# Page loads of the first two cached batches, released by groups of prompt score heads

## The chip, the cores and the metric

The kernel runs on one core of one Trainium2 chip. The metric is the device time of one execution in microseconds (us); lower is better. A core has a matrix engine (PE, TensorE), a vector engine (DVE), a scalar engine (ACT), a general engine (POOL, GpSimd) and a queue engine (SP), each with its own in-order instruction stream. They meet only at semaphores. SBUF is the on-chip memory (128 partitions), PSUM the accumulators of PE (8 banks).

## The reference, cut to what matters

One inference step of two layers. Layer 0 mixes tokens by multi-head latent attention, layer 1 by gated linear attention, and each has a feed-forward half before and after. 512 prompt tokens and 8 sample batches of 8 new tokens go through the same weights. The change lies in layer 0's attention, between these two parts:

```python
# prompt: 512 queries x 512 keys, 8 heads
s = (jnp.einsum('bqhd,bkhd->bhqk', qn, k_nope)
     + jnp.einsum('bqhr,bkr->bhqk', qp, k_pe)).astype(jnp.float32) * MLA_SCALE
p = jax.nn.softmax(s, axis=-1)
o = jnp.einsum('bhqk,bkhd->bqhd', p, v)
...
# sample: every batch reads 16 pages of 128 cached positions through its page table
past_ckv = cache_ckv[page_table].reshape(B, -1, MLA_KV_LORA)   # 256 wide
past_kpe = cache_kpe[page_table].reshape(B, -1, MLA_ROPE)      # 64 wide
```

## The kernel before, in words

Six stages run in turn: feed-forward, `mla`, feed-forward, feed-forward, `gla`, feed-forward. Activations lie transposed in SBUF; weights stream through four slots `raw`, which SP loads, ACT and POOL split into high and low parts, and PE multiplies three times (lines 1550 to 1552).

The `mla` stage has projections, then the prompt attention, then the sample attention, then the output product. In the prompt attention PE works through 32 windows (8 heads `hd` of 4 query blocks). For window `w` it computes `scores(w)` from `qn[:, hd]`, `kn[:, hd]` and `qpe[:, hd]` (lines 1789, 1790, the last raises `s_s`), DVE and ACT do the softmax (DVE lines 1245, 1248, 1250, 1255, 1258, ACT line 708), PE transposes the probabilities `prob` (line 1815), ACT copies them to `pt` (line 720), and once a head PE multiplies with the values `vp` (line 1797, which raises `s_o`). The scores run two windows ahead of the transposes.

In the sample attention the 8 batches go in 4 pairs `bp`. A batch has 16 pages of 128 positions x 320 numbers, 160 KB each, and four buffers `cache0` to `cache3` hold two pairs. A pair is worked in 4 groups `g` of 4 pages. PE transposes one batch's group (lines 1844 and 1847, `transpose_pages(x)`, x counting batch-groups: 0 and 1 are group 0 of batches 0 and 1, 2 and 3 are group 1, and so on, 8 a pair), ACT (line 734) and DVE (line 1268) copy it out, PE computes the group's scores (lines 1860, 1862); after four groups come the exponentials, their transposes (`fill`, line 1883) and the product with the pages (line 1916, which raises `s_pvg` once a group).

The buffers overlay what is dead by then. `qn` begins at `g_at` and takes 8 rows of `W4` = 2304 bytes per partition, one a head; `qpe` takes the next 8; `kn` and then `vp` follow. `cache0` takes bytes 0 to 20479 from `g_at`, `cache1` 20480 to 40959, so these two lie on `qn`, `qpe` and the first two heads of `kn`; `cache2` and `cache3` lie on the rest of `kn`, on `vp` and on what is beyond.

Each page is one DMA. SP issues two pages of every group of four, POOL the other two, both through `load_pages`, a loop that reads the page number from `table` and issues. PE waits, before a group's transposes, for all of its pages (lines 1835, 1836). Ahead of `load_pages` in SP's stream stand the weight loads up to the third block of the output product; behind it stand the load of `uv_f` and the other output weights. On POOL the splits of the projections' weights stand ahead and those of the output weights behind.

Of the kernel before, what the change touches and what calls it, by code (L numbers as in the profile page):

```python
# [27 lines left out]
HEADS, NOPE, ROPE, VD = 8, 128, 64, 128  # L28
Q_LORA, KV_LORA = 384, 256
QT, KT = Q_LORA // P, KV_LORA // P  # L30
N_POOL, PAGE, PAST = 160, 128, 2048
PAGES = PAST // PAGE
# [3 lines left out]
QB = SEQ // P  # L36
# [31 lines left out]
def hybrid_step(nc, io, stages=STAGES):  # L68
    pre_gain = PRE_GAIN
    post_gain = [None] + POST_GAIN  # L70
    with ExitStack() as ctx:
        def sem(name):
            return ctx.enter_context(nc.semaphore(name))
# [46 lines left out]
        W4 = TOK * 4  # L120
# [115 lines left out]
        s_out = sem("s_out")  # L236
# [5 lines left out]
        s_s, s_msk, s_max, s_neg = sem("s_s"), sem("s_msk"), sem("s_max"), sem("s_neg")  # L242
        s_exp, s_rec, s_pn, s_t, s_pt = sem("s_exp"), sem("s_rec"), sem("s_pn"), sem("s_t"), sem("s_pt")
        s_o, s_ohi, s_olo = sem("s_o"), sem("s_ohi"), sem("s_olo")
# [7 lines left out]
        s_pvg, s_rowt, s_rows, s_ckvs, s_masks = (sem(x) for x in ("s_pvg", "s_rowt", "s_rows", "s_ckvs", "s_masks"))  # L252
# [108 lines left out]
        def load_pages(eng, u0, landed, lo, hi):  # L361

            eng.wait_ge(s_table, 16)

            eng.wait_ge(s_o, HEADS)
            eng.wait_ge(s_evicted, u0 + M_O)
            eng.wait_ge(s_qpes, HEADS)
            eng.wait_ge(s_ckvs, 1)
            eng.wait_ge(s_out, 32)
            for bp in range(PAIRS):  # L370
                for g in range(GROUPS):
                    if 2 * bp >= CACHES:

                        eng.wait_ge(s_pvg, GROUPS * (bp - CACHES // 2) + g + 1)
                    for b in (2 * bp, 2 * bp + 1):
                        with eng.Fori(lo, hi) as i:
                            page = eng.value_load(table[0:1, bass.ds(PAGES * b + 4 * g + i, 1)], min_val=0,
                                                  max_val=N_POOL - 1)
                            eng.dma_start(cache[b % CACHES][:, 4 * g + i, :],  # L379
                                          io["cache"][page]).then_inc(landed[bp % (CACHES // 2)][g], 16)  # L380
# [28 lines left out]
        def _(sp):  # L409
# [33 lines left out]
            def mla(st):  # L443
# [25 lines left out]
                for j in range(MLA_IN + HEADS, MLA_BLOCKS - DT + SLOTS - 1):  # L469
                    load_n(j)  # L470

                load_pages(sp, u0, s_cache, 0, SP_PAGES)

                sp.wait_ge(s_pvg, GROUPS * (PAIRS - 1))
# [396 lines left out]
        def _(pool):  # L871
# [22 lines left out]
            def mla(st):  # L894
                n0 = first_block[st]
                pool.wait_ge(s_lo, n0 + SLOTS)
                for j in range(4, MLA_BLOCKS - DT):
                    low(n0 + j)
                load_pages(pool, first_unit[st], s_cache_p, SP_PAGES, 4)
                for j in range(MLA_BLOCKS - DT, MLA_BLOCKS - DT + 3):  # L900
                    low(n0 + j)
                mix_out(st, n0 + MLA_BLOCKS - DT)
# [1302 lines left out]
```

## Time and profile before

| | |
|---|---|
| median of 3 runs | 2523.54 us (2517.78 to 2524.62) |
| the profiled execution, its own time | 2515.44 us |
| its span in the trace | 2513.8 us |
| PE busy | 2439.3 us, 97% of the span |
| DVE, ACT, POOL busy | 1019.4, 789.8, 852.2 us |
| granted PE clock, mean | 0.99 |

The span runs from the first to the last instruction; the execution's own time is 1.6 us longer. All times inside the program are from the start of the span. The views of the trace used below are the page's summary, a table of stretches (busy time of each engine, granted clock and DMA share), the engines' timelines, the chain that ended last, the waits, and the groups of instructions by shape.

### The profile page before, as it was taken

The page shows a single profiled execution, that of the slowest core. Times are in us where ns is not written, and L with a number is a line of the kernel's source. Part 1 is how long each engine was busy: PE and PEld are TensorE (multiplying, and loading weights), DVE is VectorE, ACT ScalarE, POOL GpSimd, SP SyncE. Part 2 cuts the span into 40 slices and gives each one's busy share as a digit, 9 for nine tenths or more (in the row PEclk, how much of TensorE's full clock was granted, in tenths as well). Part 3 has the DMA queues.
Part 4 walks back from the last instruction along what each step waited for, and adds up shares of the span by engine and source line. Part 5 has one row for each costly group of instructions (what it writes and reads, how often), then busy time and mean ns, then how long its engine had stood idle before and what let it go on. Part 6 is the DMA issues. An engine that isn't in the chain of part 4 may idle for free.

```text
span 2513.8 us, 43938 instructions
## 1 busy us (share of the span) xinstructions
PE 2439.3 (97%) x17572; PEld 2299.7 (91%) x17572; DVE 1019.4 (41%) x1919; ACT 789.8 (31%) x1392; POOL 852.2 (34%) x477
## 2 busy tenths in 40 slices
PE   8999999899899999999999999999999999999997
PEld 8999999895456999999999999999988799999997
DVE  5332222686332643332254332126577666323223
ACT  5222222414332442222243222224321444222221
POOL 3333333120221133333314333331467423333332
PEclk9999999999999999999999999999999999999999
DMA  3222222130551232222213222222211322222222
GB/s 123 84 84 83 80 84 80 58 115 1 164 172 34 60 91 80 81 83 85 82 58 96 84 80 81 83 86 78 68 51 51 143 85 68 84 83 83 79 86 76
DMA packets 68648, 209.04 MB, mean 83 GB/s; under 512 B 8380, under 2 KB 21181, under 8 KB 68254
## 3 DMA queue, kind: packets, MB, share of 16 engines
q1 hardware_dynamic: 65438, 196.58, 25.5%
q0 software_dynamic: 3072, 10.49, 1.5%
q8 instruction: 103, 1.69, 0.3%
q14 instruction: 35, 0.29, 0.0%
HBM read 199.22 MB, written 7.82 MB: 82 GB/s over the span
## 4 chain that ended last, share of the span: by engine, by line
PE 88%; DVE 8%; ACT 1%; issue 1%; POOL 1%; DMA 0%; POOLq 0%; SPq 0%; DVEq 0%
PE psum L1550 25%; PE psum L1552 25%; PE psum L1551 25%; PE psum L1844 1%; PE psum L1860 1%; DVE h L1016 1%; PE psum L1916 1%; DVE y_ffn L1012 1%; PE psum L1998 1%; DVE x_lo L986 1%; PE psum L1790 1%; DVE work L1007 1%; PE psum L1789 1%; PE psum L1797 1%; DVE w_lo L995 1%
## 5 line engine op out<-in xcount | busy, mean ns | idle before, releaser
L875 POOL TENSOR_TENSOR w_lo<-raw,w_hi 128x1024 fp32r<-128x1024 f32 (+2 forms) x315 | 734.7, 2334 | 1420.0 <-ACT w_hi L526 1420.0
L1550 PE MATMUL psum<-x_hi,w_hi 128*128 128x288 f32 x3568 | 1072.9, 301 | 21.9 <-DVE x_lo L986 17.7
L1552 PE MATMUL psum<-x_hi,w_lo 128*128 128x288 f32 x3568 | 1053.9, 295 | 0.0
L1551 PE MATMUL psum<-x_lo,w_hi 128*128 128x288 f32 x3568 | 1052.9, 295 | 0.0
L1550 PEld LDWEIGHTS psum<-x_hi,w_hi 128*128 128x128 f32 x3568 | 671.7, 188 | 38.5 <-DVE x_lo L986 27.4
L1551 PEld LDWEIGHTS psum<-x_lo,w_hi 128*128 128x128 f32 x3568 | 671.9, 188 | 3.7
L1552 PEld LDWEIGHTS psum<-x_hi,w_lo 128*128 128x128 f32 x3568 | 671.4, 188 | 0.0
L526 ACT ACTIVATE w_hi<-raw 128x1024 fp32r<-128x1024 f32 (+2 forms) x331 | 341.4, 1033 | 797.9 <-DMA raw<-ffn_in 364.2
L1032 DVE TENSOR_TENSOR work<-psum,r_pre 128x288 f32<-128x288 f32 x352 | 160.3, 457 | 659.5 <-PE psum L1552 659.0
L1550 PE MATMUL psum<-gu_hi,w_hi 128*128 128x288 f32 x1408 | 415.5, 295 | 0.0
L1552 PE MATMUL psum<-gu_hi,w_lo 128*128 128x288 f32 x1408 | 414.7, 295 | 0.0
L1551 PE MATMUL psum<-gu_lo,w_hi 128*128 128x288 f32 x1408 | 414.6, 294 | 0.0
L1550 PEld LDWEIGHTS psum<-gu_hi,w_hi 128*128 128x128 f32 x1408 | 264.2, 188 | 0.2
L1551 PEld LDWEIGHTS psum<-gu_lo,w_hi 128*128 128x128 f32 x1408 | 264.1, 188 | 0.2
L1552 PEld LDWEIGHTS psum<-gu_hi,w_lo 128*128 128x128 f32 x1408 | 264.1, 188 | 0.0
L1037 DVE COPY y_ffn<-psum 128x288 f32 (+1 forms) x60 | 27.1, 452 | 366.9 <-PE psum L1552 366.9
L565 ACT ACTIVATE gu_hi<-work 128x288 f32 (+1 forms) x176 | 76.9, 437 | 224.6 <-DVE work L1053 224.6
L1053 DVE TENSOR_TENSOR work<-work 128x288 f32<-128x288 f32 x176 | 116.0, 659 | 28.6 <-ACT work L561 11.5
L561 ACT ACTIVATE work<-work 128x288 f32<-128x288 f32 x176 | 76.3, 436 | 134.0 <-DVE work L1032 133.9
L1048 DVE TENSOR_TENSOR acc<-acc,work 128x288 f32<-128x288 f32 x68 | 89.7, 1319 | 67.2 <-ACT work L570 67.2
L1057 DVE TENSOR_TENSOR gu_lo<-work,gu_hi 128x288 f32 (+1 forms) x176 | 79.3, 453 | 27.8 <-ACT gu_hi L565 26.1
L379 POOL DMA_DIRECT2D cache<-cache x64 | 34.5, 539 | 163.9 <-issue 162.9
(262 smaller groups left out, 1928.4 us busy)
## 6 DMA issues: line engine op xcount, KB each, us to landing
raw<-ffn_in SPq DMA_DIRECT2D x176, 512.0 KB, 3.6
raw<-ffn_out SPq DMA_DIRECT2D x64, 448.0 KB, 3.3
raw<-ffn_out SPq DMA_DIRECT2D x32, 512.0 KB, 3.5
raw<-gla_in SPq DMA_DIRECT2D x25, 512.0 KB, 3.6
cache<-cache SPq DMA_DIRECT2D x64, 160.0 KB, 3.0
cache<-cache POOLq DMA_DIRECT2D x64, 160.0 KB, 3.1
raw<-mla_wo SPq DMA_DIRECT2D x8, 512.0 KB, 3.6
raw<-gla_wo SPq DMA_DIRECT2D x8, 512.0 KB, 3.5
```

What stands on the lines that cost most here:

```text
L379: eng.dma_start(cache[b % CACHES][:, 4 * g + i, :], io["cache"][page]).then_inc(landed[bp % (CACHES // 2)][g], 16)
L526: act.activation(w_hi[slot][:, 0:w], raw[slot][:, 0:w], ACT.Copy).then_inc(s_hi, 1)
L561: act.activation(work[:, hf, :], work[:, hf, :], ACT.Silu).then_inc(s_silu, 1)
L565: act.activation(gu_hi[:, i, H[hf]], work[:, 2 + hf, :], ACT.Copy).then_inc(s_guhi, 1)
L875: pool.tensor_tensor(w_lo[slot][:, 0:w], raw[slot][:, 0:w], w_hi[slot][:, 0:w].bitcast(F32), ALU.subtract).then_inc(s_lo, 1)
L1032: dve.tensor_tensor(dst, bank[bk][0:r, 0:HALF], r_pre[0:r, H[hf]], ALU.mult).then_inc(s_evicted, 1)
L1048: dve.tensor_tensor(acc[:, H[hf]], acc[:, H[hf]], work[:, hf, :], ALU.add).then_inc(s_acc, 1)
L1053: dve.tensor_tensor(work[:, 2 + hf, :], work[:, hf, :], work[:, 2 + hf, :], ALU.mult).then_inc(s_gu, 1)
L1057: dve.tensor_tensor(gu_lo[:, pi, H[hf]], work[:, 2 + hf, :], gu_hi[:, pi, H[hf]].bitcast(F32), ALU.subtract).then_inc(s_gulo, 1)
L1550: pe.matmul(out, wh, xh, start=start, stop=False)
L1551: pe.matmul(out, wh, xl, start=False, stop=False)
L1552: return pe.matmul(out, wl, xh, start=False, stop=stop)
```

## The change

The six waits that stood ahead of all page loads are split. Three of them (`s_table`, `s_evicted`, `s_qpes`) stay where they were. The other three (`s_o` at 8 heads, `s_ckvs`, `s_out`) move to the first load of batch 2. Each group's loads of batches 0 and 1 get a wait of their own, on the number of prompt score windows done.

```diff
-            eng.wait_ge(s_o, HEADS)
             eng.wait_ge(s_evicted, u0 + M_O)
             eng.wait_ge(s_qpes, HEADS)
-            eng.wait_ge(s_ckvs, 1)
-            eng.wait_ge(s_out, 32)
+
+            def last_head(b, g):
+
+                page_w = (KV_LORA + ROPE) * 4
+                held = range((b * PAGES + 4 * g) * page_w // W4, ((b * PAGES + 4 * g + 4) * page_w - 1) // W4 + 1)
+                return max(x % HEADS if x < 2 * HEADS else HEADS - 1 for x in held)
+
             for bp in range(PAIRS):
                 for g in range(GROUPS):
                     if 2 * bp >= CACHES:
 
                         eng.wait_ge(s_pvg, GROUPS * (bp - CACHES // 2) + g + 1)
                     for b in (2 * bp, 2 * bp + 1):
+                        if b < 2:
+                            eng.wait_ge(s_s, QB * (last_head(b, g) + 1))
+                        if (b, g) == (2, 0):
+                            eng.wait_ge(s_o, HEADS)
+                            eng.wait_ge(s_ckvs, 1)
+                            eng.wait_ge(s_out, 32)
                         with eng.Fori(lo, hi) as i:
```

In the order of issue, (group 0, batch 0), (0, 1), (1, 0), (1, 1), (2, 0), (2, 1), (3, 0), (3, 1), the new waits are for `s_s` at 12, 16, 20, 24, 28, 32, 32, 32 of 32 windows.

POOL's stream before, at the start of the page loads (`w_lo`, `raw`, `w_hi` are slots of the last projection weights; `cache_107` and `cache_108` are `cache0` and `cache1`, `cache_109` and `cache_110` are `cache2` and `cache3`):

```order
L875 TENSOR_TENSOR w_lo_59<-raw_55,w_hi_63 128x1024 [waits s_hi]
L376 UNCONDITIONAL_BRANCH [waits s_qpes,s_ckvs,s_evicted,s_out,s_o,s_table]
L376 ISA
L377 TENSOR_LOAD table
L377 ISA x2
L379 ISA
L379 DMA cache_107<-cache 128x320
L376 REGISTER_ALU
L376 COMPARE_AND_BRANCH
L376 UNCONDITIONAL_BRANCH
```

The same place of POOL's stream in the change:

```order
L885 TENSOR_TENSOR w_lo_59<-raw_55,w_hi_63 128x1024 [waits s_hi]
L386 UNCONDITIONAL_BRANCH [waits s_qpes,s_s,s_evicted,s_table]
L386 ISA
L387 TENSOR_LOAD table
L387 ISA x2
L389 ISA
L389 DMA cache_107<-cache 128x320
L386 REGISTER_ALU
L386 COMPARE_AND_BRANCH
L386 UNCONDITIONAL_BRANCH [waits s_s]
```

No instruction is added or moved: each loop's first branch now carries the wait for `s_s`, and `s_o`, `s_ckvs` and `s_out` are gone from the first. SP's stream changes in the same way, and the streams of PE, DVE and ACT are what they were.

POOL's stream in the change at the last load of batch 1 and the first of batch 2:

```order
L386 UNCONDITIONAL_BRANCH [waits s_s]
L386 ISA
L387 TENSOR_LOAD table
L387 ISA x2
L389 ISA
L389 DMA cache_108<-cache 128x320
L386 REGISTER_ALU
L386 COMPARE_AND_BRANCH
L386 UNCONDITIONAL_BRANCH [waits s_out,s_ckvs,s_o]
```

Here the three waits have come to stand, ahead of `cache_109`; in the kernel before this last branch had no wait.

## Rows read from the trace of the kernel before

**Rows 1.** The page, chain that ended last, shares by engine

```profile
PE 88%; DVE 8%; ACT 1%; issue 1%; POOL 1%; DMA 0%; POOLq 0%; SPq 0%; DVEq 0%
```

**Rows 2.** Stretches: us, busy PE, PEld, DVE, ACT, POOL; clock, DMA share, GB/s

```profile
646.00:648.00 2.00, 0.00 (x0) 0.00 (x0) 0.00 (x0) 0.00 (x0) 0.92 (x2) 0.50 0.70 215
...
654.00:656.00 2.00, 1.95 (x10) 1.39 (x8) 0.69 (x1) 0.63 (x3) 0.79 (x2) 0.51 0.74 234
656.00:658.00 2.00, 1.47 (x12) 1.26 (x12) 0.69 (x1) 0.94 (x2) 0.54 (x1) 1.00 0.63 202
```

**Rows 3.** PE timeline, prompt attention to pair 0: start, duration, instruction, idle before

```profile
588.50 1.12 PE L1790 MATMUL psum<-kpe,qpe 64*128 64x512 f32 x2
...
633.40 1.12 PE L1790 MATMUL psum<-kpe,qpe 64*128 64x512 f32 x2
...
638.70 2.42 PE L1797 MATMUL psum<-pt,vp 128*128 128x512 f32 x8 [0.69 <-ACT pt L720]
642.54 0.41 PE L1827 MATMUL psum<-ident,ckv_s 128*64 128x128 f32 x2 [1.41 <-DVE x_lo L1236]
650.60 1.94 PE L1844 MATMUL psum<-ident,cache 128*128 128x128 f32 x8 [7.65 <-DMA cache<-cache]
...
656.53 1.06 PE L1844 MATMUL psum<-ident,cache 128*128 128x128 f32 x8 [0.58 <-issue]
...
662.92 1.06 PE L1844 MATMUL psum<-ident,cache 128*128 128x128 f32 x8 [0.51 <-issue]
...
680.54 2.66 PE L1883 MATMUL psum<-ident,p_s 128*128 128x128 f32 x16 [0.37 <-ACT p_s L748]
```

**Rows 4.** PE timeline, last product of pair 0 and pair 1

```profile
684.44 7.13 PE L1916 MATMUL psum<-cache,pt_s 128*64 128x256 f32 x64
...
692.08 1.09 PE L1844 MATMUL psum<-ident,cache 128*128 128x128 f32 x8
...
695.04 1.94 PE L1860 MATMUL psum<-c_t,q_lat 128*64 128x512 f32 x8
...
713.19 1.09 PE L1844 MATMUL psum<-ident,cache 128*128 128x128 f32 x8
...
715.60 2.66 PE L1883 MATMUL psum<-ident,p_s 128*128 128x128 f32 x16 [0.37 <-ACT p_s L748]
```

**Rows 5.** POOL timeline, page issues: 1st, 4th, 8th and 33rd of 64

```profile
643.00 0.74 POOL L379 DMA_DIRECT2D cache<-cache  x1 [94.50 <-issue]
...
647.62 0.54 POOL L379 DMA_DIRECT2D cache<-cache  x1 [1.00 <-issue]
...
653.72 0.54 POOL L379 DMA_DIRECT2D cache<-cache  x1 [1.01 <-issue]
...
692.42 0.54 POOL L379 DMA_DIRECT2D cache<-cache  x1 [0.99 <-PE psum L1916]
```

**Rows 6.** Chain that ended last, in time, at the first pages

```profile
647.62 2.84 DMA cache<-cache
```

**Rows 7.** SP's waits between 560 and 800 us: total, times, longest

```profile
SPq L369 <- PE psum L1797: 72.4, 1, 72.4
```

**Rows 8.** Groups by shape, 575 to 640 us: busy, mean ns, idle before

```profile
L1815 PEld LDWEIGHTS psum<-ident,prob 128*128 128x128 f32 x75 | 8.1, 140 | 12.6 <-DVE prob L1258 11.3 <-issue 0.5
...
L1248 DVE TENSOR_REDUCE soft<-psum 128x1 f32<-128x512 f32 x7 | 4.8, 691 | 0.2
...
L1258 DVE TENSOR_SCALAR prob<-prob,soft 128x512 f32<-128x512 f32 x8 | 3.9, 487 | 0.3
```

**Rows 9.** Groups by shape, DVE, 642 to 750 us

```profile
L1292 DVE TENSOR_REDUCE mx<-psum 128x1 f32<-128x512 f32 x12 | 8.3, 692 | 32.3 <-PE psum L1862 32.3
```

**Rows 10.** Groups by shape, DVE, feed-forward, 200 to 450 us

```profile
L1048 DVE TENSOR_TENSOR acc<-acc,work 128x288 f32<-128x288 f32 x12 | 15.5, 1291 | 11.3 <-ACT work L570 11.3
...
L1016 DVE TENSOR_TENSOR h<-h,y_ffn 128x288 f32<-128x288 f32 x8 | 3.6, 456 | 0.0
```

**Rows 11.** PE timeline, pair 3

```profile
785.74 3.58 PE L1883 MATMUL psum<-ident,p_s 128*128 128x128 f32 x16 [0.37 <-ACT p_s L748]
```

## The prediction, made before the changed kernel had run

> **What bounds the kernel now.** First the chain that ended last: 88% of the span is PE's own work [rows 1], so a change pays only where PE stands still or runs slowly. The changed waits hold back page loads, so I went next to the place where PE meets the first pages. PE's timeline shows the last value product of the prompt attention, from 638.70 to 641.12, then 1.41 us of idleness and two small transposes that end at 642.95, and then 7.65 us in which PE waits for a page DMA [rows 3]. Seek three things there. The first is that hole. The second is in the table of stretches: in the hole the granted clock falls to 0.50, that is from 2.4 to 1.2 GHz, it is still 0.51 at 654 to 656 us, and it is 1.00 again from 656 us [rows 2]. The third is two gaps, 0.58 us before 656.53 and 0.51 us before 662.92, both before a new group's transposes [rows 3].
>
> What is late in all of them is POOL's share of the pages. POOL issues its first page at 643.00, 1.9 us after the last value product ended, the fourth at 647.62 and the eighth at 653.72 [rows 5], so one each 1.53 us ((653.72 - 643.00) / 7). The chain names the fourth POOL issue and 2.84 us to its landing [rows 6]: group 0 is complete at 650.46, and PE starts at 650.60. Group 1 is complete at 653.72 + 2.84 = 656.56, and PE starts its next group at 656.53. Group 2 comes four issues later, about 662.7, against 662.92. So the two "issue" gaps are page waits too. Group 3 would land at about 668.8. From there on PE is not held by pages: pair 1 shows no gap before its transposes [rows 4].
>
> **The change part by part.** No instruction is added; eight waits for `s_s` on each of two queues cost nothing, since these stand still anyway (SP has waited 72.4 us for the value products [rows 7]). All that changes is when the loads may start.
>
> *Batches 0 and 1.* PE's rows date the semaphore: the fourth window of head 2 ends at 588.50 + 1.12 = 589.6 and that of head 7 at 633.40 + 1.12 = 634.5, five heads apart, so a head takes 8.98 us [rows 3]. The waits at 12, 16, 20, 24, 28 and 32 windows open at 589.6, 598.6, 607.6, 616.5, 625.5 and 634.5. POOL's first issue comes 1.9 us later. Groups 0 and 1 and half of group 2 lie in SBUF before 634.5. Then POOL has six issues left: the first at 636.4, the last at 636.4 + 5 x 1.53 = 644.1, landed at 646.9.
>
> *What PE then does.* It ends the small transposes at 642.95 and goes straight on, at the full clock. Two batch-groups of transposes take 695.04 - 692.08 = 2.96 us in pair 1 [rows 4], and from the first of these, the ones of the pair's second group, it is 715.60 - 692.08 = 23.52 us to the fills [rows 4]. Pair 0 first has its group 0 and then this same stretch. For pair 0: 642.95 + 2.96 = 645.91, + 23.52 = 669.43, against 680.54 now [rows 3]: **11.1 us** earlier. By terms: 7.65 us of hole; the first two batch-groups took 656.53 - 0.58 - 650.60 = 5.35 us instead of 2.96, so 2.4 us of half clock; and 0.58 + 0.51 = 1.1 us of gaps. Sum 11.1 us, both ways.
>
> *What is late next.* Group 3 is needed three groups of work after the start, about 658, and is there at 646.9. Batch 2 and 3 loads now queue behind the six late issues: POOL gets to them at 645.6. Before, they were the 17th issue, at 643.00 + 16 x 1.53 = 667.5, so they come 22 us earlier. Their group 0 has landed at about 645.6 + 3 x 1.53 + 2.84 = 653.0. PE wants it where x 8 is transposed. That is the counterpart of 713.19 in pair 1, one pair period (715.60 - 680.54 = 35.1 us) earlier and 11.1 us shifted, so 667.0: 14 us to spare. Their 16 issues end near 668.5. Pair 2 needs the first quarter of pair 0's product, at 684.44 + 1.8 - 11.1 = 675.1. POOL is free by then, where before it reached this load only at 692.42 [rows 4, 5]. It lands near 684 and is wanted at 713.19 - 11.1 = 702.1. Pair 3 has the same relation to pair 1's product as before. No new page wait follows, and what comes after (`uv_f`, output weights) hangs on semaphores of the sample attention and shifts with it. All later stages start 11.1 us earlier.
>
> *What I can't read off.* POOL now issues 16 page DMAs while DVE and ACT do the prompt softmax. PE is full there, but not by a wide margin: its weight loads waited 11.3 us in all for DVE's scaled `prob` [rows 8], so a late DVE operation reaches PE almost at once. The lower bound of the cost is 0: DVE's maximum over 512 columns takes 691 ns in the quiet attention [rows 8] and 692 ns while pages stream [rows 9], so the traffic alone stretches nothing. The upper bound: each of the 16 issues holds up a DVE operation for its whole 0.54 us [rows 5], 8.6 us. That POOL and DVE can hurt each other is in the feed-forward: the same 128x288 add takes 1291 ns as `acc` and 456 ns as `h` [rows 10]. I take 0.2 us, since POOL's issues follow a head's last score by 1.9 us and 3.4 us, and the `prob` scaling is on for only 0.49 us each time [rows 8]; this is the nearest to the lower end.
>
> A rule of the Trainium skill speaks against the change at this point. Its page "SBUF — State Buffer", section "Who interferes with whom", says that a tensor_scalar in a two-port mode and GpSimd's writing of descriptors for its DMAs lock each other out for a whole instruction. No row shows the two together, since before the change POOL issued nothing in the attention. By the rule alone the sum would lie between 11.1 and 2.5 us, depending on how often they meet.
>
> *The clock.* The fills of pair 3 took 3.58 us [rows 11], those of pair 1 2.66 us [rows 4], so the clock was low once more near 785 us. With everything shifted by 11 us this may come or not come there, or in one of the other short gaps at the end of the stage. I count 0.9 us either way.
>
> **Sum.** 11.1 - 0.2 = 10.9 us. The profiled execution has 2515.44 us and would have 2504.5. It is 8.1 us under the median of the runs shown, so I put the saving on the median: 2523.54 - 10.9 = 2512.6 us, ratio 0.9957.
>
> **The rivals.** (1) *The port.* DVE and POOL meet, and PE's chain stretches by 3 to 8.6 us. For it: the add of 1291 ns [rows 10]. Against: few meetings, and the two engines must coincide within half a microsecond. Time 2515.5 to 2521. (2) *The wait only moves.* The pages are there, but PE is then held by the copies of ACT and DVE, or pair 1 waits for its pages. Against: pair 1 does the same work at 23.52 us with no gap [rows 4], and 14 us are spare. If pair 0 kept its old length from first transpose to fill (680.54 - 650.60 = 29.94 us), only the hole would be won: 2523.5 - 7.7 = 2515.9. (3) *Slower.* The streaming pages stretch the attention itself, by PE's operand reads or all engines. From 589.6 to 641.1 it has 51.5 us; it loses the 11.1 us from a stretch of 22% on and is slower by over 0.3% from 36% (18.7 us) on; 40% would give 2523.5 + 20.6 - 11.1 = 2533. Against: the equal 691 and 692 ns [rows 8, 9]. (4) *It does nothing*, as when a wait stays behind another queue entry. Against: in both streams only the loads stand there, and the kept waits were met before the attention. 2523.5.
>
> **How the numbers follow.** Forecast 0.76, port 0.10, moved wait 0.08, nothing 0.03, slower 0.03. A measurement of this kernel tells about 0.3%, 7.6 us, from no change. The forecast is past it by 3.3 us, and the shown runs are 6.8 us apart, so I leave it a few in a hundred on the wrong side: faster 0.79, same 0.18, slower 0.03. The range: down to 2504 for runs that fall as low as the profiled one (2504.5), up to 2520 for most of the port's cases and the moved wait.
>
> **What would show it.** Right: page issues on SP and POOL from about 591 us in five steps of 9 us; PE's transposes of `cache` start at 643 with no DMA wait; the clock stays at 1.00 between 642 and 658; fills of pair 0 at about 669.4; 8.98 us a head as before. Wrong: a head period above 9.0 us, DVE lines 1258 or POOL's issues longer than 487 and 540 ns, a DMA wait at x 8, or a new clock drop.

## The result, and the profile after

The changed kernel takes 2509.56 us (median of 4 runs, 2509.07 to 2510.05), the kernel before in the same session 2524.08 us (median of 4, 2517.78 to 2525.13). The ratio is 0.9946, with a 95% interval of 0.9933 to 0.9959. That is a saving of 14.5 us between the medians and of 13.6 us by the ratio, where 10.9 us were forecast; the forecast ratio of 0.9957 lies inside the interval. The profiled execution took 2509.59 us with a span of 2507.9 us.

PE's timeline of the changed kernel at the places of [rows 3] and [rows 4] (start, duration, instruction, idle before; the change moves line numbers by 10):

```profile
591.72 1.12 PE L1800 MATMUL psum<-kpe,qpe 64*128 64x512 f32 x2
...
636.62 1.12 PE L1800 MATMUL psum<-kpe,qpe 64*128 64x512 f32 x2
...
641.93 2.42 PE L1807 MATMUL psum<-pt,vp 128*128 128x512 f32 x8 [0.69 <-ACT pt L730]
645.76 0.41 PE L1837 MATMUL psum<-ident,ckv_s 128*64 128x128 f32 x2 [1.41 <-DVE x_lo L1246]
646.01 1.04 PE L1854 MATMUL psum<-ident,cache 128*128 128x128 f32 x8
...
649.05 1.06 PE L1854 MATMUL psum<-ident,cache 128*128 128x128 f32 x8
...
654.86 1.09 PE L1854 MATMUL psum<-ident,cache 128*128 128x128 f32 x8
...
670.14 1.09 PE L1854 MATMUL psum<-ident,cache 128*128 128x128 f32 x8
...
672.54 2.66 PE L1893 MATMUL psum<-ident,p_s 128*128 128x128 f32 x16 [0.37 <-ACT p_s L758]
...
707.61 2.66 PE L1893 MATMUL psum<-ident,p_s 128*128 128x128 f32 x16 [0.37 <-ACT p_s L758]
```

The hole of 7.65 us and both small gaps are gone; PE goes from the small transposes straight to the pages. The stage before the attention happened to run 3.2 us later than in the profile of before, so I measure from inside: from the start of the last value product to the fills of pair 0 it is 672.54 - 641.93 = 30.61 us, against 680.54 - 638.70 = 41.84 [rows 3]. This stretch is called **the page stretch** below. It is 11.2 us shorter. The heads take (636.62 - 591.72) / 5 = 8.98 us as before, and the pairs 35.1 us.

POOL's timeline shows the page issues: the first of group 0 for batch 0 and for batch 1, the first after the last score, and the first issues of batch 2 and of pair 2 (that is, of batches 4 and 5).

```profile
594.76 0.74 POOL L389 DMA_DIRECT2D cache<-cache  x1 [43.99 <-issue]
...
603.27 0.54 POOL L389 DMA_DIRECT2D cache<-cache  x1 [6.40 <-issue]
...
639.19 0.54 POOL L389 DMA_DIRECT2D cache<-cache  x1 [6.92 <-issue]
...
648.47 0.54 POOL L389 DMA_DIRECT2D cache<-cache  x1 [1.08 <-issue]
...
679.84 0.54 POOL L389 DMA_DIRECT2D cache<-cache  x1 [7.34 <-issue]
```

The first issue comes 1.9 us after the twelfth window's score (591.72 + 1.12). The later waits cost less: the last one opens at 636.62 + 1.12 = 637.74 and its issue follows 1.45 us later. The table of stretches (us; busy PE, PEld, DVE, ACT, POOL; granted clock, DMA share, GB/s) has the full clock where [rows 2] had half of it:

```profile
646.00:648.00 2.00, 1.93 (x18) 1.69 (x17) 1.11 (x2) 0.92 (x2) 0.54 (x1) 1.00 0.73 230
654.00:656.00 2.00, 2.00 (x14) 1.19 (x13) 1.00 (x2) 0.01 (x1) 0.54 (x1) 1.00 0.71 209
```

What remained open was the difference between 11.2 us in the page stretch and 13 to 14.5 us in the medians of this run and its repeat (e3). The intervals of both ratios hold the 0.9956 that 11.2 us alone would give, so no single run shows that difference clear of the noise. All runs together do suggest it: 86 executions of the kernel before, in five sessions, have a mean of 2522.5 us and the nine of the change one of 2509.5, which is 13.0 us.

### The profile page after: what moved, and what is told of

Same layout as the page of the kernel before. It is cut to its first block, busy times and chain, and to the rows that moved or that the text cites. A ratio compares the mean times of both kernels' runs of the same rounds, so it can differ in the third digit from the quotient of the medians.

```text
span 2507.9 us, 43938 instructions
## 1 busy us (share of the span) xinstructions
PE 2440.0 (97%) x17572; PEld 2300.2 (92%) x17572; DVE 1021.7 (41%) x1919; ACT 789.6 (31%) x1392; POOL 852.7 (34%) x477
## 4 chain that ended last, share of the span: by engine, by line
PE 88%; DVE 8%; ACT 1%; POOL 1%; issue 1%; DMA 0%; SPq 0%; DVEq 0%; POOLq 0%
PE psum L1560 25%; PE psum L1562 25%; PE psum L1561 25%; PE psum L1870 1%; PE psum L1854 1%; DVE h L1026 1%; PE psum L1926 1%; DVE y_ffn L1022 1%; DVE x_lo L996 1%; PE psum L1800 1%; DVE work L1017 1%; PE psum L2008 1%; PE psum L1799 1%; PE psum L1807 1%; DVE w_lo L1005 1%
## 5 line engine op out<-in xcount | busy, mean ns | idle before, releaser
L1560 PEld LDWEIGHTS psum<-x_hi,w_hi 128*128 128x128 f32 x3568 | 672.4, 188 | 37.6 <-DVE x_lo L996 27.4
L1063 DVE TENSOR_TENSOR work<-work 128x288 f32<-128x288 f32 x176 | 116.2, 660 | 28.3 <-ACT work L571 11.2
```

Of the source, the lines that this page charges most:

```text
L1063: dve.tensor_tensor(work[:, 2 + hf, :], work[:, hf, :], work[:, 2 + hf, :], ALU.mult).then_inc(s_gu, 1)
L1560: pe.matmul(out, wh, xh, start=start, stop=False)
```

## The experiments

Beside the page stretch a second length turned out to matter, **the stage's end**: from the start of the fills of pair 3 to the first matmul of line 1578 (line numbers of the kernel before), a sum of squares near the end of the output product; the expectations call it the first sum of squares. It holds the same work in all kernels but e10 and e11, which have more. The two lengths are read from one profiled execution of each kernel, the medians from all executions. The ratios are not quotients of the medians; for e12 these would give 0.9974. All times in us:

| kernel | median | ratio to before, 95% | page stretch | stage's end |
|---|---|---|---|---|
| before, the profile of [rows 3] | | | 41.84 | 64.3 |
| the change | 2509.56 | 0.9946 [0.9933, 0.9959] | 30.61 | 66.4 |
| e1, before again | 2522.65 | 1.0004 [0.9994, 1.0014] | 42.04 | 70.1 |
| e2, same streams, late loads | 2524.92 | 1.0006 [0.9997, 1.0016] | 42.21 | 70.1 |
| e3, the change again | 2509.07 | 0.9952 [0.9937, 0.9966] | 30.63 | 65.8 |
| e4, one release | 2517.46 | 0.9978 [0.9968, 0.9989] | 36.53 | 70.0 |
| e5, first group only | 2519.61 | 0.9984 [0.9971, 0.9997] | 37.63 | 70.1 |
| e6, POOL issues all | 2508.78 | 0.9952 [0.9938, 0.9966] | 30.62 | 65.8 |
| e7, before, hole filled | 2522.55 | 0.9998 [0.9986, 1.0011] | 42.42 | 68.8 |
| e8, change + 80 transposes | 2520.28 | 0.9991 [0.9978, 1.0004] | 39.36 | 64.3 |
| e9, change + 40 | 2515.93 | 0.9967 [0.9952, 0.9983] | 34.99 | 68.8 |
| e12, change + 20 | 2516.64 | 0.9966 [0.9952, 0.9980] | 32.81 | 70.1 |
| e10, change, end gaps filled | 2507.72 | 0.9940 [0.9923, 0.9956] | 30.63 | 63.3 |
| e11, before, end gaps filled | 2519.94 | 0.9990 [0.9979, 1.0001] | 42.63 | 63.3 |

**e1: the kernel before against itself.** No edit.

> The kernel before, unchanged, timed against itself. Theory (the change saves some 11 us and what the medians show beyond that, 14.5 us, is the scatter of whole executions): ratio 1.000 within 0.002, but single runs between about 2515 and 2525 us, and the stretch from the start of the last value product (line 1797) to the fills of pair 0 (line 1883) stays at 41.8 us whatever the whole time is. Rival (the kernel before is always near 2524 and the profiled 2515 was a freak): all runs within 2 us of 2524.

The kernel before scattered from 2518.35 to 2526.91 us, so the profile of before, at 2515.44, was a low one. Its span here is 2522.7 us, 8.9 more. That splits up: 1.3 ahead of the attention, 0.2 in the page stretch, 5.8 at the stage's end, and 1.6 after it. The page stretch hardly moves; the rest does.

**e2: the streams of the change without the early start.**

```diff
                     for b in (2 * bp, 2 * bp + 1):
+                        if (b, g) == (0, 0):
+                            eng.wait_ge(s_o, HEADS)
                         if b < 2:
```

> The change, but the first page load also waits for all eight heads' value products, so that no load starts earlier than before; the instruction streams are those of the change. Theory (only the earlier start pays): ratio 1.000, last value product to fills 41.8 us as before. Rival (the other shape of the streams is itself worth the 3 us by which the medians exceed the sum): about 2521 us, ratio 0.9987, with the difference ahead of the prompt attention.

Nothing is won, neither in time nor in the page stretch. The gain needs the early loads; the shape of the streams gives none that shows.

**e3: the change again.** No edit.

> The change itself, timed again in more rounds. Theory: last value product to fills 30.6 us, 11.2 less than before, ratio near 0.9956. Rival (some 3 us more are really won elsewhere): ratio 0.9945 or lower, and a second place in the trace where it is always shorter than the kernel before.

The page stretch is 30.63 us, and the five runs lie within 3 us (2507.87 to 2510.79), where those of the kernel before spread over 11 (2516.59 to 2527.41). The ratio came out as 0.9952 with 0.9956 inside its interval, so this run alone leaves both theories standing. The trace has the second place, the stage's end.

**e4: one release for all eight groups.**

```diff
                         if b < 2:
-                            eng.wait_ge(s_s, QB * (last_head(b, g) + 1))
+                            eng.wait_ge(s_s, ATT)
```

> The change, but all eight groups of batches 0 and 1 wait for the scores of all 32 windows, not head by head. POOL would start 1.9 us after 634.5 on the clock of the kernel before, one issue each 1.53 us: group 0 landed at 643.8, group 1 at 650.0. Theory (issue pace of POOL bounds what an early start is worth): PE waits 4.1 us for group 1, fills at 673.5, stretch 34.8 us, saving about 7 us, ratio 0.9972. Rival (releasing by heads is unneeded, one release at the last score hides it all): stretch 30.6 us, ratio as the change.

In PE's timeline of e4 the first pages and the second group:

```profile
647.41 1.29 PE L1854 MATMUL psum<-ident,cache 128*128 128x128 f32 x8 [0.64 <-DMA cache<-cache]
...
654.08 1.13 PE L1854 MATMUL psum<-ident,cache 128*128 128x128 f32 x8 [2.18 <-issue]
```

PE waits 0.64 us for group 0 and 2.18 us for group 1, and the clock falls to half twice (0.53 at 648 to 650 us, 0.50 at 656 to 658 us), so the stretch is 36.5 us and not 34.8. Half of the page gain is kept (42.0 - 36.5 = 5.5 of 11.4 us). The other half needs the release head by head, since POOL issues only one page each 1.53 us.

**e5: only the first group released by heads.**

```diff
+                        if (b, g) == (0, 1):
+                            eng.wait_ge(s_o, HEADS)
```

> The change, but only the first group of batches 0 and 1 is released by scores; group 1 and all later ones wait for the eight value products as before. Theory (POOL's pace): group 1 lands at 650.5 on the clock of the kernel before, PE waits 4.6 us for it after the first two transposes, fills at 674.0, stretch from last value product to fills 35.3 us, saving 6.5 us, ratio 0.9974. Rival (the 7.65 us hole was only a start-up cost, so one early group removes it all): stretch 30.6 us.

PE's timeline of e5, from group 0 to group 1:

```profile
643.45 1.04 PE L1856 MATMUL psum<-ident,cache 128*128 128x128 f32 x8
...
645.00 1.06 PE L1856 MATMUL psum<-ident,cache 128*128 128x128 f32 x8
...
651.13 1.94 PE L1856 MATMUL psum<-ident,cache 128*128 128x128 f32 x8 [4.64 <-DMA cache<-cache]
```

The wait for group 1 is 4.64 us, forecast 4.6. After it the clock is low, seen in the eight transposes of 1.94 us, which I had left out: 37.6 us and not 35.3. The hole is the pace of the issues and no start-up cost. It comes back at the first group that isn't early.

**e6: POOL issues all pages of batches 0 and 1.** The wait counts of the two page semaphores follow.

```diff
+                        if b < 2 and lo == 0:
+                            continue
-                        with eng.Fori(lo, hi) as i:
+                        with eng.Fori(0 if b < 2 else lo, hi) as i:
```

> The change, but POOL alone issues all pages of batches 0 and 1, 32 issues instead of 16 during and after the prompt scores; SP issues none of them. Theory (POOL's descriptor work costs DVE's softmax nothing here): a head still takes 8.98 us, line 1258's scaling of 512 columns 487 ns, pages still early enough, ratio as the change, about 0.9956. Rival (POOL and DVE shut each other out): heads of 9.1 us or more in which POOL issues, up to 17 us lost by 32 x 0.54 us, POOL issues longer than 0.54 us.

With twice the issues the page stretch, the head's 8.98 us and the time are those of the change. The timeline of e6 has an issue that runs across a scaling of `prob`:

```profile
611.51 0.42 DVE L1270 TENSOR_SCALAR prob<-prob,soft 128x384 f32<-128x384 f32 x1
611.59 0.54 POOL L391 DMA_DIRECT2D cache<-cache  x1 [3.83 <-issue]
```

Both have the durations that they have alone: 421 ns is this scaling's mean in the kernel before, where POOL issued nothing in the attention, and 0.54 us is the issue of [rows 5]. Such meetings are common. In e6 13 scalings of `prob` meet an issue, and in four of them the issue began first (607.23 us, the scaling of 128 columns at 607.35); that scaling takes 0.29 us with a meeting and without. In the change itself five of the issues meet a scaling of 384 columns, again of 0.42 us. The pages also land no later: 2.4 us after the issue at 611.59 and 2.4 us after that at 641.65, which meets no operation of DVE. The mean over 512 columns in e6:

```profile
L1270 DVE TENSOR_SCALAR prob<-prob,soft 128x512 f32<-128x512 f32 x8 | 3.9, 486 | 0.3
```

It was 487 ns before [rows 8]. The port rival falls.

**e7: the kernel before with PE busy in the hole.**

```diff
+                for i in range(48):
+                    pe.transpose(bank[5][:, i % 4 * P:(i % 4 + 1) * P], ident[:, :], ident[:, :])
                 transpose_pages(0)
```

> The kernel before, but PE does 48 transposes of the identity into an unused bank (6.4 us) in the hole in which it waits for the first pages; the loads are as before. Theory (2.4 us of the 11.1 are the half clock that follows the idleness): the clock stays at 1.00 from 642 to 658 us, the first two batch-groups take 3.0 instead of 5.35 us, the stretch is 39.4 us, saving 2.4 us, ratio 0.9990. Rival (the transposes were slow for another reason, such as the landing pages): 5.35 us again and a stretch of 41.8 us.

My theory failed here, twice over. PE's timeline of e7:

```profile
654.02 1.26 PE L1844 MATMUL psum<-ident,cache 128*128 128x128 f32 x8 [2.31 <-DMA cache<-cache]
...
655.93 1.91 PE L1844 MATMUL psum<-ident,cache 128*128 128x128 f32 x8
...
659.83 1.06 PE L1844 MATMUL psum<-ident,cache 128*128 128x128 f32 x8 [1.33 <-issue]
```

After the remaining 2.31 us of waiting the clock still fell, only later (0.69 at 654 to 656 us, 0.50 at 656 to 658). So the run is no test of a clock that stays full. And the 0.9 us that the first two batch-groups did win (658.50 - 654.02 = 4.48 us instead of 5.35) went almost whole into a longer wait for group 1, 1.33 us instead of 0.58 [rows 3], since group 1 lands when POOL has issued it. Group 1's transposes start 659.83 - 642.22 = 17.6 us after the last value product begins; in the kernel before it was 656.53 - 638.70 = 17.8 [rows 3].

**e8, e9 and e12: the change, delayed.** 80, 40 and 20 transposes of the identity ahead of `transpose_pages(0)`, added to the change as in e7.

> The change, with 80 added transposes of the identity (10.6 us of PE work at full clock) ahead of the first page transposes, so that all after it runs as late as in the kernel before, but without the idle hole. The question is what makes the last 4 us: from the fills of pair 3 to the first sum of squares of the next stage it is 70.1 us in the runs of the kernel before and its undone forms, 65.8 to 66.4 us in the three profiles of the change. Theory (the full-clock history matters, the idle hole near 645 us leads to the long half-clock stretch near 805): 66 us here, time the change's plus 10.6, about 2519.7 us. Rival (only the position in time matters): 70 us, about 2523.7 us.

> As the run with 80 added transposes, with 40 (5.3 us). Theory (history): 66 us from the fills of pair 3 to the first sum of squares, about 2514.4 us. Rival (position in time): some other length between 64 and 70 us, and a time that is not the change's plus 5.3.

> The change with 20 added transposes (2.65 us of PE work) ahead of the first pages. Of the kernels run so far all but the change and its all-POOL form lie on one line, 2523 us minus what the stretch from the last value product to the fills of pair 0 is shorter than 42.0 us, within 1.1 us (36.5 us: 2517.5; 35.0: 2515.9; 39.4: 2520.3); the change lies some 2 us under it. Here the stretch is 33.3 us. Theory (the 2 us belong to the place in time at which the change's later gaps fall): back on the line, 2514.3 us, with runs spread over more than 5 us. Rival (they belong to the change, which has no idle hole): 2509.3 + 2.65 = 2512.0 us and runs within 3 us.

Against 2509.3 us (the middle of the change's two medians), the medians rise by 11.0, 6.6 and 7.3 us for page stretches longer by 8.8, 4.4 and 2.2 us. (The expectations counted 0.13 us for each added transpose, but PE's timeline shows 48 of them in 5.40 us in e7 and 80 in 8.90 us in e8, 0.11 us each.) The runs are wide apart in all three (2513.76 to 2524.03, 2512.67 to 2518.88, 2506.39 to 2517.85). The smallest delay costs 5 us more than its own work in the median, and one run of it is the fastest of all, 2506.39. So a missing hole isn't enough to keep the end short: e12 has no hole and an end of 70.1 us. That goes against the history theory, though e8's median is within 1 us of what it forecast (with the 8.8 us that its transposes really took, the theory gives 2518.1 and the median is 2.2 us above). The opposite one, that a place in time fixes the length, expected 70 us and 2523.7 us of e8, which gave 64.3 and 2520.28; of e12 it had the wide spread right and the median too low by 2.3 us. Neither holds as it was put.

The single executions show why medians mislead here. Those of e5 form two groups with nothing between them: four at 2512.77 to 2514.35 us with a granted clock of 0.991 or 0.992, and six at 2519.26 to 2521.80 us with 0.988. In e12 two lie at 2506.39 and 2509.76 (0.993, 0.992) and six at 2516.09 to 2517.85 (0.989); in e8 five lie at 2513.76 to 2518.59 (0.992, 0.993) and five at 2521.96 to 2524.03 (0.988, 0.989), and the median of e8, 2520.28, falls where no execution does. The profiled executions of e5 and e12 belong to the upper groups and have an end of 70.1 us; that of e8 belongs to the lower group and has 64.3. So the table's last column tells as much about which execution was profiled as about the kernel, and the 5 us of e12 beyond its own work go with six of eight executions being in the upper group. The means of the groups lie 6.9, 8.8 and 7.2 us apart in e5, e12 and e8. The difference of the ends, 70.1 - 64.3 = 5.8 us, would be most of that. But this is read from three profiles and isn't shown for the executions without one.

**e10 and e11: the gaps at the stage's end filled.** Transposes of the identity into bank 6, 12 after the last scores, 5 and 7 around line 1927, 10 ahead of the output product, in the change (e10) and in the kernel before (e11).

```diff
+                busy(10)
                 pe.wait_ge(s_olo, HEADS + 1)
```

> The change, with transposes of the identity into an unused bank in the four short gaps at the end of the sample attention (12, 5, 7 and 10 of them, each a little shorter than its gap of 1.7, 0.7, 1.0 and 1.4 us). Theory (the short gaps let the clock fall, which costs 2 to 6 us at the stage's end): the clock stays at 1.00 from 775 to 815 us, fills of pair 3 to the first sum of squares 64.3 us, 1.5 to 2 us faster than the change, ratio to the kernel before 0.9944. Rival (the fall has another cause, or the added work is in the way): 66 us or more.

> The kernel before with the same transposes in the four gaps at the stage's end. Theory: 64.3 us instead of 70.1 from the fills of pair 3 to the first sum of squares, so up to 5.8 us faster than the kernel before, ratio 0.998, and the distance to the change with the same transposes is the 11.2 us of the pages alone. Rival (the excess over 11.2 us is not the clock at the stage's end): no gain, distance 13 to 14 us.

PE's timeline at the stage's end, of e1:

```profile
787.20 3.49 PE L1883 MATMUL psum<-ident,p_s 128*128 128x128 f32 x16 [0.37 <-ACT p_s L748]
...
801.43 7.00 PE L1933 MATMUL psum<-o_lat,uv_f 128*128 128x64 f32 x32 [1.03 <-DVE o_lat L1323]
...
857.30 0.65 PE L1578 MATMUL psum<-work,ones 128*128 128x288 f32 x2
```

and of e11:

```profile
789.26 2.66 PE L1887 MATMUL psum<-ident,p_s 128*128 128x128 f32 x16 [0.36 <-ACT p_s L748]
...
802.28 3.79 PE L1941 MATMUL psum<-o_lat,uv_f 128*128 128x64 f32 x32 [0.18 <-DVE o_lat L1323]
...
852.55 0.65 PE L1578 MATMUL psum<-work,ones 128*128 128x288 f32 x2
```

The same 32 matmuls take 7.00 us and 3.79 us. The table of stretches of e1 has the reason:

```profile
802.00:804.00 2.00, 2.00 (x12) 2.00 (x11) 0.00 (x0) 0.00 (x0) 0.00 (x0) 0.50 0.00 0
...
812.00:814.00 2.00, 2.00 (x10) 2.00 (x10) 0.00 (x0) 0.00 (x0) 0.46 (x1) 0.50 0.00 0
```

From 802 to 814 us PE runs at 1.2 GHz, 0.50, and is busy all that time but for one gap of 1.4 us. Gaps of 1.7, 0.7 and 1.0 us lie in the 18 us before. With the gaps filled the clock is 1.00 from 776 to 826 us and the end is 63.3 us in both kernels. Without filling, the two shortest ends, 64.3 us, had the full clock at this place too, and half of it only at the fills of pair 3 (before and e8; 3.58 us in [rows 11] instead of 2.66). In the medians e11 is 4.5 us under the 2524.48 us of the kernel before in its session, but its ratio of 0.9990 has 1 inside the interval (0.9979 to 1.0001), so this gain isn't clear of the noise. Its executions do lie closer together, within 5.8 us against 10.5. e10 is 1.6 us under the change, measured in other sessions. The distance of e10 and e11, measured in one session, is 12.2 us; without the filling the medians are 13.2 to 14.5 us apart (14.5 for the change, 13.2 for e3, 14.4 for e6, each against the kernel before in its session). The page stretches of the two profiles differ by 12.0. That is what one would see if the excess were the clock at the stage's end, but these differences are no larger than the intervals.

## Why the prediction was right, point by point

*What bounds.* Right: the wait was for the pages, group by group, and POOL's share came last. e5 shows it at its purest: first group early, and the wait of 4.64 us stands before the second, where the pace of 1.53 us had put it. But POOL's share is late by little. SP's timeline of the kernel before:

```profile
642.41 16.91 SPq L379 DMA_DIRECT2D cache<-cache  x12
```

Twelve issues of 0.35 us each in 16.91 us make one each 1.5 us, (16.91 - 0.35) / 11, as on POOL, with a median of 2.4 us to landing against POOL's 2.7. By these numbers SP's half of group 0 would be complete at about 642.41 + 3 x 1.5 + 2.4 = 649.3 us (an estimate), only 1.1 us ahead of POOL's 650.46. The pace of both queues made the hole; a faster POOL alone would have won about 1 us of it.

*Batches 0 and 1, and what PE does then.* Right. 11.1 us were forecast for the page stretch, 11.2 were measured (41.84 to 30.61), and 11.4 against e1. The six late issues began 1.45 us after the last score and not 1.9, which changes nothing, since their pages were early by far. Pair 0 went from its second group to the fills in 672.54 - 649.05 = 23.49 us, forecast 23.52. No later group waited: batch 2's first transposes begin at 670.14 without idleness.

*The terms of that sum.* Their total held, their split did not. I booked 2.4 us on the half clock as if they could be won apart. In e7 a clock that was full for part of the way won 0.9 us ahead of group 1 and nothing in the page stretch (42.42 us), since group 1 isn't in SBUF before. The hole, the slow transposes and the gaps are one thing, the landing of the pages. The sum came right because it was also made from end to end, from pair 1's rows.

*The port.* 0.2 us taken, 0 measured: POOL's issues during and after the attention's scores, 16 in the change and twice that in e6, left the head at 8.98 us. The reason that I gave against the port was wrong: the meetings are not few, since five of the change's 16 issues begin 0.1 us after a scaling of `prob` and run beside it. The term came out small because a meeting costs nothing here. The rule of the Trainium skill's page "SBUF — State Buffer", section "Who interferes with whom", doesn't show itself in this case. Issue and scaling overlapped in e6 and both kept their lengths, whichever began first. The 1291 ns add of [rows 10], on which the rival leaned, is a mean of two kinds. The timelines of DVE and POOL in the kernel before:

```profile
331.99 2.11 POOL L875 TENSOR_TENSOR w_lo<-raw,w_hi 128x896 fp32r<-128x896 f32 x1 [3.36 <-ACT w_hi L526]
332.36 2.05 DVE L1048 TENSOR_TENSOR acc<-acc,work 128x288 f32<-128x288 f32 x1 [1.37 <-ACT work L570]
335.38 0.46 DVE L1048 TENSOR_TENSOR acc<-acc,work 128x288 f32<-128x288 f32 x1 [0.60 <-ACT work L570]
```

All six adds that meet a split of weights by POOL take 2.05 to 2.16 us, and the six that meet none take 0.46. So what goes with the long adds is POOL's arithmetic, of which there is none in the attention, and not its page issues; no run changed the split to prove it.

*The clock.* The step that was mis-sized. "I count 0.9 us either way" should have been some 6 us one way: with the same work the stage's end ran from 64.3 to 70.1 us, and the profile from which I read had the shortest one, so it could only get longer (66.4 us in the change's profile). For the same reason the 2504.5 us at the lower end of the range was not reached: the nine executions of the change lie between 2507.87 and 2510.79. The median came out 3.0 us under the forecast 2512.6. The page stretch gives only 0.3 us of that; the rest could only be in this term, which the sum took as nothing on balance, or in the scatter. So the mechanism was forecast, and the total was right within the width of its range. The whole excess of the medians over the page stretch is not shown piece by piece. Against e1's profile the change's has +2.0 us ahead of the last value product, -11.4 in the page stretch, -3.7 at the stage's end and -1.6 after, together the 14.8 us between the spans. In the profiles of e10 and e11, with the end's gaps filled, the third part is gone.

*What stays open:* why all nine timed runs of the change and the five of e6 fall in a narrow band (2507.87 to 2510.79), while 20 transposes more spread the runs over 11 us. The delays suggest that the position in time has a part in it, and show that the missing hole isn't enough. What makes a position good isn't found; each profile is also a single execution.

## What to carry to other kernels

A load that overwrites several dead buffers should wait for the last reader of each piece, not of the whole. How early it must start follows from the pace of the slower issuing queue (here 1.53 us a page), so count issues times pace before choosing the release: one release at the last score kept only half of the gain. Make a sum of a stall from end to end against a stretch of the same work without it. Its parts, hole and slow clock and small gaps, need not be separable. And where a kernel's runs scatter by 0.4%, compare one inner stretch of the profiles first, and look at the single times before trusting a median: it can lie between two groups, and it carries clock falls of other stages with it.

## What the runs showed of the hardware that was not expected

After short gaps of PE, of 0.7 and 1.0 us, the clock can stay at half for 12 us although PE is busy in most of them (e1), or not fall at all (the profile of before, where the same 32 matmuls took 3.76 us). It differs between executions of one kernel. With useless transposes in the gaps the median is 1.6 us lower than the change's, which makes e10 the fastest version in the median, though its interval overlaps the change's. The Trainium skill's page "TensorE: Matmul & The Clock Gate", section "Part 1: The HAM clock gate", says that the point at which the clock goes up varies by about half a microsecond from run to run. That is too little for what the traces show: in e1 PE is busy without a gap for the 7.00 us of those 32 matmuls and the clock is 0.50 from 802 us on, while in the profile of before it is 1.00 throughout. Here the measurement decides.
